# Last attention's bias stored once a query and added on GpSimd, and the last product split over two engines

## The chip, the cores and the metric

The kernel runs on one core of a Trainium2 chip, as one program in one launch. The metric is the device time of a whole execution, in microseconds (us), as the median of several executions. The engines are named as the profile names them: PE is the tensor engine (PEld its weight load), DVE the vector engine, ACT the scalar engine, POOL is GpSimd, and SP is the engine that issues the DMAs (SPq its queue).

## What is computed

Two blocks, one behind the other, in float32, for one sequence of 256 tokens of 1024 features. The first has two layers with grouped attention, neighbourhood attention and gates. The second has a feed-forward stage, a mixer, another feed-forward stage and an embedding step, and ends in an RMS norm. The change touches one part of the mixer, and the last norm. Cut to these:

```python
def dsa_attention(q, c_kv, q_idx, k_idx, w_idx, rel_bias):
    # per block of 128 queries
    score = jnp.einsum('bths,bth->bts', jax.nn.relu(dots), w)
    score = jnp.where(causal[None], score, -jnp.inf)
    _, sel = lax.top_k(score, top_k)                    # 64 keys of each query
    bias = rel_bias[t5_bucket(q_pos[None, :, None] - sel)]
    logits = einsum('bthc,btkc->bthk', qb, kv_sel) * (dc ** -0.5) + bias
    logits = jnp.where(valid, logits, -jnp.inf)
    probs = jax.nn.softmax(logits, axis=-1)
    return jnp.einsum('bthk,btkc->bthc', probs, kv_sel)

def rms_norm_2(x, g):
    return x * lax.rsqrt(jnp.mean(x * x, axis=-1, keepdims=True) + EPS) * g

def second_block(...):
    ...
    hn = rms_norm_2(h, ple_norm[i])
    h = h + jax.nn.sigmoid(hn @ ple_w_gate[i]) * (p[i] @ ple_w_proj[i])
    return rms_norm_2(h, final_norm)
```

The bias of a head depends only on the distance of query and key, and there are 8 heads (SH).

## The kernel before

**Weights.** All large weights come as one stream of units of 128x2048 numbers (`load_unit`, L691), which SP loads into a ring of three buffers `raw`. For each unit ACT makes `w_hi`, the rounded weights (`cut_to`, L831), and DVE or POOL makes `w_lo = raw - w_hi` in four pieces of 128x512 (DVE: `lo_to`, L1265; POOL: L814, for the units named in `POOLS`, among them "iq", "ms" and "yg"). PE multiplies three times for each block (hi x hi, hi x lo, lo x hi, L1988; for "gv" L2270) and so makes a "line", one tile of 128 features by 256 tokens. Most units hold two lines. A unit is loaded when `w_lo` of the unit three before it is done; its `w_hi` is made when PE is done with the lines of the unit three before it.

**Order.** Each engine has its own program, written out by hand, and runs it in order; the engines meet only at semaphores. In ACT's program, `cut_to(u)` stands at fixed places among other work and makes `w_hi` up to unit u.

**The bias row.** PE computes the bias by distance for 8 heads as one 8x512 tile, ACT copies it to `bias_row`, 8 partitions of `turned`. SP stores it to DRAM as `row_dram`, 8 rows of 2 KB (L750), behind the load of the unit of lines gv6 and gv7; the next load is that of unit iq0 (lines iq0 and iq1). In the stage of the levels that follows, PE makes the lines gv0 to gv7 and iq0 to iq3 two by two, with other products between them; ACT copies each gv line out of its bank (L1098), and PE's line gv(n+2) waits for the copy of gv(n).

**The choice.** `choose(t)` on DVE, for each of two query tiles t, keeps 64 keys of each query (MAX8 and MATCH_REPLACE8) and leaves `score[:, t]`, 0 for a chosen key and -1e30 for others.

**The last attention.** 16 jobs, (head, query tile), with 128 keys for tile 0 and 256 for tile 1. For job i:
- SP has loaded the bias of the head into one of two buffers `rbias` (`load_rbias`, L716). The source rows overlap: row p is `row_dram` shifted by p numbers, so the queries come in reversed order.
- PE: `dsa_scores(i)`, the score product (L2353), and onto it the product of the constant "flip" with `rbias` (L2355), which turns the order of the queries.
- DVE: `dsa_maxes(i)`, adds `score` (L1863), then the maximum, negated (L1864).
- ACT: `dsa_exps(i)`, the exponential with its sum (L1175).
- DVE: `dsa_shares(i)`, reciprocal (L1870) and normalisation (L1871).
- PE: `dsa_turn(i)`, transposes into the bank `turn` (L2364); ACT: `dsa_turned(i)` copies it out (L1183); PE: `dsa_values(i)` (L2373); ACT and DVE split the result of a head into hi and lo.

Between these run the lines of `DSA_FILLERS`: ms0 to ms7 in jobs 0 to 7, yg0 to yg7 in jobs 8 to 15. PE's order in step i is: score i, line i, turn i-1, values i-2. ACT's is: exponential i, then `cut_to` the unit two ahead of that of line i (so in even steps a `w_hi` of 1.9 us), for an "ms" line its tanh, then the copy of turn i-1. DVE's is: maximum i, shares i, the scaling or gating of line i (which frees its bank), and the lo part of a head.

**The end.** For each of 8 lines "pg", DVE scales the line, and one step later makes the new `h` (`embedded(m)`), ACT squares it, DVE adds the squares (`add_square`, L1304). PE sums over the partitions (`norm_sum`, L2016), ACT takes Ln and Exp, DVE makes three small steps (L1290, L1281, L1282) for the root's reciprocal and then eight products `wide = h * g * r` (L1951). SP stores them in four DMAs (L762).

```python
        def dsa_scores(i):
            ...
            pe.matmul(bank[:, 0:keys], dq[:, hd, t * P:(t + 1) * P], ckv[:, 0:keys], start=True, stop=False)
            pe.wait_ge(rbias_in[hd % 2], 16 * TILES * (hd // 2 + 1))
            pe.matmul(bank[:, 0:keys], const("flip"), rbias[:, hd % 2, t * P:t * P + keys], start=False,
                      stop=True).then_inc(score_done, 1)
```

Of the kernel before, what the change touches and what calls it, by code (L numbers as in the profile page):

```python
# [317 lines left out]
CONST, CONST_W = columns([("ident", P), ("flip", P), ("head_mean", P),  # L318
# [169 lines left out]
def hybrid_blocks_kernel(nc, weights, tokens, embeds, small_in, small2_in, rpb, consts_in, consts2_in, levels_in,  # L488
# [87 lines left out]
    rbias_in = [sem(f"rbias_in{i}") for i in range(2)]  # L576
# [8 lines left out]
    dq_ready, relued, scored = sem("dq_ready"), sem("relued"), sem("scored")  # L585
    od_hi_ready, od_ready = sem("od_hi_ready"), sem("od_ready")
# [4 lines left out]
    stored = sem("stored")  # L591

# [17 lines left out]
    row_dram = nc.dram_tensor("bias_by_distance", (SH, 2 * SEQ), F32).ap()  # L610
# [62 lines left out]
    rbias = a4.sb("rbias", [2, SEQ + P])  # L673
# [3 lines left out]
    bias_row = turned[0:SH].rearrange("p a b -> p (a b)")[:, SEQ:3 * SEQ]  # L677
    a3.close()
# [6 lines left out]
    def _(sp):  # L685
# [22 lines left out]
        def load_rbias(hd):  # L708

            if hd >= 2:  # L710

                sp.wait_ge(score_done, SCORE[("mixer", "dsa", hd - 2, TILES - 1)] + 1)
# [12 lines left out]
        for u in range(1, NU):  # L725
# [34 lines left out]
        for k in range(0, KT, 2):  # L760
            sp.wait_ge(out_ready, k + 2)
# [5 lines left out]
    def _(pool):  # L767
# [30 lines left out]

        means = False
# [16 lines left out]


    @block.scalar
    def _(act):
# [350 lines left out]
        def dsa_exps(i):  # L1170
# [5 lines left out]
                           accum_out=total[:, n % 2, 0:1]).then_inc(exped, 1)  # L1176
# [44 lines left out]

        def square_of_result(k):
# [3 lines left out]
        for m in range(KT):  # L1226
# [6 lines left out]
            if m:  # L1233
                square_of_result(m - 1)
        square_of_result(KT - 1)
        load_log_table(False)
# [4 lines left out]
    def _(dve):  # L1241
# [35 lines left out]
        def newton(r, v, mean, out_=None):  # L1277
# [4 lines left out]
            link(dve.scalar_tensor_tensor(r if out_ is None else out_, v, -3.0, r, ALU.add, ALU.mult))  # L1282

        def rstd_of(key, n, out_=None):
# [8 lines left out]
            newton(r, v, mean, out_)  # L1293
# [532 lines left out]
        def choose(t):  # L1826
# [13 lines left out]
            link(dve.tensor_tensor(own, own, const("later"), ALU.add))  # L1840
# [96 lines left out]
        for m in range(KT):  # L1937
# [612 lines left out]
```

## Time and profile before

| | |
|---|---|
| median of 3 executions | 1202.46 us (1201.43 to 1204.3) |
| profiled execution | 1199.7 us, its span 1197.9 us |
| mean granted clock of PE | 0.993 |
| PE busy in the span | 1149.3 us, 96% |
| DVE, ACT, POOL busy | 829.4, 602.7, 255.5 us |
| moved by DMA | 188.05 MB, 157 GB/s on average |

The profile is of one execution. Its span is the time between the first and the last instruction; the execution's own time is 1.8 us longer. A time such as "at 861.3" is counted from the span's start. In a row of the timeline the two first numbers are start and duration in us. Operations on one engine overlap a little: the next starts before the last one's end. A bracket at a row's end says how long the engine was idle before it and which operation ended that.

### The profile page before, as it was taken

To read this page: it belongs to the slowest core of one execution; us is meant where nothing else is said; L and a number is where in the kernel's file an instruction comes from. 1 tells how busy PE (TensorE), PEld (TensorE's weight loads), DVE (VectorE), ACT (ScalarE), POOL (GpSimd) and SP (SyncE) were. 2 spreads that over 40 slices of the span, in tenths; PEclk is the share of its full clock that TensorE was granted. 3 is DMA by queue.
4 is the path that set the end of the run, shared out by engine and by line. 5 is a ranking of instruction groups with operands and counts; after the bars stand their busy time and mean duration, and the time that the engine had idled before them with its cause. 6 is when DMAs were issued, how large, how long until landed. Compare 5 with 4: busy or idle time off the path is not lost.

```text
span 1197.9 us, 23145 instructions
## 1 busy us (share of the span) xinstructions
PE 1149.3 (96%) x9278; PEld 1121.2 (94%) x9278; DVE 829.4 (69%) x1801; ACT 602.7 (50%) x941; POOL 255.5 (21%) x213
## 2 busy tenths in 40 slices
PE   6999999999999998999999999999999999999996
PEld 6999999999999998999999899888899999999995
DVE  6954445879445477887766799577846877776667
ACT  6454545554555546454444553565454554444453
POOL 1065543200756514000000008300561000000000
PEclk9999999999999999999999999999999999999998
DMA  6743353356533633555455443224464555554551
GB/s 241 177 183 126 107 129 108 140 165 166 188 129 112 164 114 141 194 206 182 155 178 194 178 176 142 106 72 154 150 166 147 185 177 177 189 187 148 191 201 36
DMA packets 47978, 188.05 MB, mean 157 GB/s; under 512 B 20856, under 2 KB 24184, under 8 KB 29312
## 3 DMA queue, kind: packets, MB, share of 16 engines
q1 hardware_dynamic: 47872, 186.58, 46.7%
q8 instruction: 74, 1.21, 0.4%
q14 instruction: 32, 0.26, 0.1%
HBM read 185.50 MB, written 1.06 MB: 156 GB/s over the span
## 4 chain that ended last, share of the span: by engine, by line
PE 78%; DVE 14%; ACT 3%; issue 2%; DMA 1%; POOL 0%; SPq 0%; DVEq 0%; ACTq 0%
PE line L1988 48%; PE result L1988 17%; DVE w_lo L1265 4%; PE line L2270 1%; PE turn L2117 1%; PE result L2151 1%; ACT w_hi L831 1%; PE stat L2151 1%; PE score L2098 1%; PE score L2287 1%; PE score L2094 1%; DMA raw<-in_weights 1%; DMA rel<-in_rpb 1%; DVE wide L1547 1%; DVE prod L1544 1%
## 5 line engine op out<-in xcount | busy, mean ns | idle before, releaser
L831 ACT ACTIVATE w_hi<-raw 128x2048 fp32r<-128x2048 f32 (+2 forms) x178 | 321.9, 1810 | 112.6 <-PE line L1988 41.0
L814 POOL TENSOR_TENSOR w_lo<-raw,w_hi 128x512 fp32r<-128x512 f32 x168 | 227.5, 1386 | 572.5 <-ACT w_hi L831 572.5
L1265 DVE TENSOR_TENSOR w_lo<-raw,w_hi 128x512 fp32r<-128x512 f32 (+2 forms) x544 | 337.3, 665 | 4.8 <-ACT w_hi L864 2.6
L1988 PE MATMUL line<-x_hi,w_hi 128*128 128x256 f32 (+1 forms) x1080 | 320.0, 296 | 12.7 <-DVE x_lo L1311 8.5
L1988 PE MATMUL line<-x_hi,w_lo 128*128 128x256 f32 (+1 forms) x1080 | 308.3, 285 | 0.0
L1988 PE MATMUL line<-x_lo,w_hi 128*128 128x256 f32 (+1 forms) x1080 | 307.9, 285 | 0.0
L1988 PEld LDWEIGHTS line<-x_hi,w_hi 128*128 128x128 f32 x1080 | 205.7, 190 | 19.2 <-issue 13.0
L1988 PEld LDWEIGHTS line<-x_lo,w_hi 128*128 128x128 f32 x1080 | 205.2, 190 | 1.7
L1988 PEld LDWEIGHTS line<-x_hi,w_lo 128*128 128x128 f32 x1080 | 205.6, 190 | 0.0
L1988 PE MATMUL line<-y_hi,w_hi 128*128 128x256 f32 (+1 forms) x688 | 203.8, 296 | 1.8 <-DVE y_lo L1520 1.2
L1988 PE MATMUL line<-y_hi,w_lo 128*128 128x256 f32 (+1 forms) x688 | 194.7, 283 | 0.0
L1988 PE MATMUL line<-y_lo,w_hi 128*128 128x256 f32 (+1 forms) x688 | 194.4, 283 | 0.0
L1988 PEld LDWEIGHTS line<-y_hi,w_hi 128*128 128x128 f32 x688 | 129.8, 189 | 3.9 <-DVE y_lo L1520 1.4
L1988 PEld LDWEIGHTS line<-y_lo,w_hi 128*128 128x128 f32 x688 | 129.6, 188 | 1.5
L1988 PEld LDWEIGHTS line<-y_hi,w_lo 128*128 128x128 f32 x688 | 130.0, 189 | 0.0
L1988 PE MATMUL result<-x_hi,w_hi 128*128 128x256 f32 (+1 forms) x232 | 65.5, 282 | 0.0
L1988 PE MATMUL result<-x_lo,w_hi 128*128 128x256 f32 (+1 forms) x232 | 65.4, 282 | 0.0
L1988 PE MATMUL result<-x_hi,w_lo 128*128 128x256 f32 (+1 forms) x232 | 65.4, 282 | 0.0
L956 ACT ACTIVATE probs<-score,top 128x272 f32<-128x272 f32 (+1 forms) x66 | 32.2, 487 | 64.0 <-DVE top L1438 36.8
L1988 PE MATMUL result<-y_lo,w_hi 128*128 128x256 f32 x192 | 54.0, 281 | 0.0
L1988 PE MATMUL result<-y_hi,w_lo 128*128 128x256 f32 x192 | 54.0, 281 | 0.0
L1988 PE MATMUL result<-y_hi,w_hi 128*128 128x256 f32 x192 | 53.9, 281 | 0.0
(335 smaller groups left out, 2193.6 us busy)
## 6 DMA issues: line engine op xcount, KB each, us to landing
raw<-in_weights SPq DMA_DIRECT2D x145, 1024.0 KB, 4.8
raw<-in_weights SPq DMA_DIRECT2D x32, 704.0 KB, 4.1
rel<-in_rpb SPq DMA_DIRECT2D x64, 64.0 KB, 6.5
h<-in_tokens SPq DMA_DIRECT2D x2, 544.0 KB, 6.0
raw<-in_weights SPq DMA_DIRECT2D x2, 512.0 KB, 5.7
rbias<-bias_by_distance SPq DMA_DIRECT2D x8, 128.0 KB, 5.6
out<-wide SPq DMA_DIRECT2D x4, 256.0 KB, 2.2
consts<-in_consts SPq DMA_DIRECT2D x1, 832.0 KB, 6.7
```

The lines of the kernel that those rows point to most:

```text
L814: pool.tensor_tensor(w_lo[:, u % CUT, at], raw[:, u % RAW, at], w_hi[:, u % CUT, at].bitcast(F32), ALU.subtract).then_inc(lo_pool, 1)
L831: act.activation(w_hi[:, v % CUT, first:n], raw[:, v % RAW, first:n], ACT.Copy).then_inc(hi_cut, 1)
L956: act.activation(probs[0:m, place % 2, half * SECOND:half * SECOND + TOK], score_bank[s % 2][0:m, 0:TOK], ACT.Exp, bias=top[0:m, n % 2, 0: ...
L1265: dve.tensor_tensor(w_lo[:, u % CUT, at], raw[:, u % RAW, at], w_hi[:, u % CUT, at].bitcast(F32), ALU.subtract).then_inc(lo_cut, 1)
L1544: dve.scalar_tensor_tensor(prod[:, m % 2, 0:W], gate["b"][:, m, 0:W], 1.0, line_wait((name, "yb", m))[:, 0:W], ALU.add, ALU.mult).then_inc ...
L1547: dve.tensor_tensor(wide[:, m, 0:W], prod[:, m % 2, 0:W], gate["a"][:, m, 0:W], ALU.add).then_inc(full_ready, 1)
L1988: ins = pe.matmul(bank[:, 0:n], stay, move[:, first + k, 0:n], start=(k, m) == (0, 0), stop=(k, m) == (depth - 1, 2))
L2094: ins = pe.matmul(s[:, 0:TOK], qa[:, c, t * P:(t + 1) * P], ka_half[:, half * TOK:(half + 1) * TOK], start=True, stop=True)
L2098: ins = pe.matmul(s[:, 0:TOK], qb[:, c, t * P:(t + 1) * P], kb[:, c, half * TOK:(half + 1) * TOK], start=True, stop=True)
L2117: ins = pe.transpose(turn_bank[:, b * P:b * P + m], probs[0:m, place, first:first + P], ident[0:m, 0:m])
L2151: ins = pe.matmul(single_bank[pair % 2][:, cols], tn[:, b * P:(b + 1) * P], v[:, kt, cols], start=(half, kt) == (0, 0), stop=b == both)
L2270: ins = pe.matmul(bank, stay[:, k], move[:, k], start=(k, m) == (0, 0), stop=(k, m) == (KT - 1, 2))
```

## The change

- The store of the bias row now writes each head's row 128 times, once for each query of a tile: `row_dram` is 8 x 128 x 384 numbers. The source is `bias_row` broadcast over the middle dimension.
- `load_rbias` reads row p of a head's table at a shift of -p, with a pitch of 383 numbers, so the queries come in their own order. There are four buffers `rbias` instead of two (`RING` is 4), and the loads of four heads are issued ahead of unit mg2 instead of two. A later load waits for the maximum of the head four before it.
- "flip" is no more: neither the product in `dsa_scores` nor the constant.
- POOL adds `score`, the choice, to `rbias` (`bias_of`), in place. In POOL's program these additions stand behind the last piece of unit ms0 + n, for n = 1 to 7 (ms0 is the unit of lines ms0 and ms1): jobs 2n-2 and 2n-1 behind unit ms0 + n, and jobs 12 to 15 behind the last.
- DVE's `dsa_maxes` waits for that addition and for the score product, and makes sum and maximum in one operation; it leaves the sum negated, so ACT's exponential takes a scale of -1. The last operation of `choose` is signalled to POOL (`chosen`).
- At the end, `embedded(m)` comes in its own step, behind the addition of the square before it; ACT also makes `hg = h * g` (`gained`), and loads its table ahead of the last square; PE sums in two products, the last one straight from ACT's square; and the eight last products become four of 128x512, three on DVE and one (features 4 and 5) on POOL, which is stored last.

```diff
-            for t in range(TILES):
-                at = hd * 2 * SEQ + SEQ - (t + 1) * P
-                src = bass.AP(row_dram.tensor, at, [[1, P], [1, (t + 1) * P]])
-                sp.dma_start(rbias[:, hd % 2, t * P:t * P + (t + 1) * P], src).then_inc(rbias_in[hd % 2], 16)
+            for t in range(TILES):
+                at = hd * P * SPREAD + SEQ - t * P - 1
+                src = bass.AP(row_dram.tensor, at, [[SPREAD - 1, P], [1, (t + 1) * P]])
+                sp.dma_start(rbias[:, hd % RING, t * P:t * P + (t + 1) * P], src).then_inc(rbias_in[hd % RING], 16)
...
-                sp.dma_start(row_dram, bias_row).then_inc(row_stored, 16)
+                sp.dma_start(row_dram, bias_row[:, 0:SPREAD].unsqueeze(1).to_broadcast([SH, P, SPREAD])).then_inc(
+                    row_stored, 16)
...
-                load_rbias(0)
-                load_rbias(1)
-            if 2 <= u - UNIT[("mixer", "ms", 0)] - 1 < SH:
+                for hd in range(RING):
+                    load_rbias(hd)
+            if RING <= u - UNIT[("mixer", "ms", 0)] - 1 < SH:
...
+        def bias_of(i):
+            hd, t = DSA_JOBS[i]
+            at = rbias[:, hd % RING, t * P:t * P + (t + 1) * P]
+            pool.wait_ge(rbias_in[hd % RING], 16 * TILES * (hd // RING + 1))
+            pool.wait_ge(chosen, t + 1)
+            pool.tensor_tensor(at, at, score[:, t, 0:(t + 1) * P], ALU.add).then_inc(chosen_bias, 1)
...
                 pool.tensor_tensor(w_lo[:, u % CUT, at], raw[:, u % RAW, at], w_hi[:, u % CUT, at].bitcast(F32),
                                    ALU.subtract).then_inc(lo_pool, 1)
+                hd = u - UNIT[("mixer", "ms", 0)]
+                if 1 <= hd < SH and end == BLOCKS[u]:
+                    for i in range(TILES * (hd - 1), TILES * (hd + (hd == SH - 1))):
+                        bias_of(i)
...
+        pool.wait_ge(hg_ready, KT)
+        pool.wait_ge(last_root, 1)
+        by = rstd[:, STAT[("final1", "norm")] % 2, 0:SEQ].unsqueeze(1).to_broadcast([P, 2, SEQ])
+        pool.tensor_tensor(wide[:, 4:6, 0:SEQ], hg[:, 4:6], by, ALU.mult).then_inc(out_pool, 1)
...
             bank = score_bank[s % 2][:, 0:keys]
+            dve.wait_ge(chosen_bias, i + 1)
             dve.wait_ge(score_done, s + 1)
-            link(dve.tensor_tensor(bank, bank, score[:, t, 0:keys], ALU.add))
-            dve.tensor_reduce(top[:, n % 2, 0:1], bank, AX.X, ALU.max, negate=True).then_inc(maxed, 1)
+            dve.tensor_tensor_reduce(bank, bank, rbias[:, hd % RING, t * P:t * P + keys], scale=-1.0, scalar=3.0e38,
+                                     op0=ALU.add, op1=ALU.min, accum_out=top[:, n % 2, 0:1]).then_inc(maxed, 1)
...
             if m:
-                embedded(m - 1)
-            if m >= 2:
-                add_square("final1", m - 2, m - 2, SEQ)
-        embedded(KT - 1)
-        add_square("final1", KT - 2, KT - 2, SEQ)
-        add_square("final1", KT - 1, KT - 1, SEQ)
-        dve.wait_ge(h_ready, H_BATCH["embed"] + KT)
-        r = rstd_of(("final1", "norm"), SEQ)
-        for k in range(KT):
-            dve.scalar_tensor_tensor(wide[:, k, 0:SEQ], h[:, k, 0:SEQ], operand("g_final1")[:, k:k + 1], r, ALU.mult,
-                                     ALU.mult).then_inc(out_ready, 1)
+                add_square("final1", m - 1, m - 1, SEQ)
+            embedded(m)
+        dve.wait_ge(hg_ready, KT)
+        r = rstd_of(("final1", "norm"), SEQ, last=True)
+        by = r.unsqueeze(1).to_broadcast([P, 2, SEQ])
+        for k in (0, 2, 6):
+            dve.tensor_tensor(wide[:, k:k + 2, 0:SEQ], hg[:, k:k + 2], by, ALU.mult).then_inc(out_ready, 1)
...
-            pe.matmul(bank[:, 0:keys], dq[:, hd, t * P:(t + 1) * P], ckv[:, 0:keys], start=True, stop=False)
-            pe.wait_ge(rbias_in[hd % 2], 16 * TILES * (hd // 2 + 1))
-            pe.matmul(bank[:, 0:keys], const("flip"), rbias[:, hd % 2, t * P:t * P + keys], start=False,
+            pe.matmul(bank[:, 0:keys], dq[:, hd, t * P:(t + 1) * P], ckv[:, 0:keys], start=True,
                       stop=True).then_inc(score_done, 1)
...
-        norm_sum("final1", SEQ)
+        pe.wait_ge(summed, SUMMED["final1"] + KT - 1)
+        pe.matmul(stat_bank[:, 0:SEQ], mean_dm[:, :], sum_of["final1"][0][:, 0:SEQ], start=True, stop=False)
+        pe.wait_ge(squares_ready, SQUARES[("final1", "norm")] + KT)
+        pe.matmul(stat_bank[:, 0:SEQ], mean_dm[:, :], square_of["final1"][:, (KT - 1) % 2, 0:SEQ], start=False,
+                  stop=True).then_inc(stat_done, 1)
```

## Rows read from the trace of the kernel before

**Rows 1.** The page: the span, and part 1, busy time of each engine.
```profile
span 1197.9 us, 23145 instructions
PE 1149.3 (96%) x9278; PEld 1121.2 (94%) x9278; DVE 829.4 (69%) x1801; ACT 602.7 (50%) x941; POOL 255.5 (21%) x213
```
**Rows 2.** Timeline, last attention: start us, us, engine, line, operation, out<-in, count.
```profile
861.10 0.40 PE L2353 MATMUL score<-ckv,wide 128*128 128x128 f32 x2
861.33 0.39 PE L2355 MATMUL score<-rbias,consts 128*128 128x128 f32 x2
...
865.24 0.60 PE L2353 MATMUL score<-ckv,wide 128*128 128x256 f32 x2
865.67 0.59 PE L2355 MATMUL score<-rbias,consts 128*128 128x256 f32 x2
```
**Rows 3.** Timeline of ACT and POOL, last attention's first jobs.
```profile
859.91 0.37 ACT L1175 ACTIVATE probs<-score,top 128x128 f32<-128x128 f32 x1 [4.71 <-DVE top L1864]
860.26 1.90 ACT L831 ACTIVATE w_hi<-raw 128x2048 fp32r<-128x2048 f32 x1
862.24 10.11 POOL L814 TENSOR_TENSOR w_lo<-raw,w_hi 128x512 fp32r<-128x512 f32 x8 [6.23 <-ACT w_hi L831]
```
**Rows 4.** One line of the kernel (L796): POOL's 128x256 additions, durations in ns.
```profile
L796 POOL TENSOR_TENSOR prod<-prod,th x14: 728/742/1257, 455.1 to 477.6; 128x256 f32<-128x256 f32 x14
```
**Rows 5.** Timeline of DVE, the first maximum.
```profile
859.25 0.30 DVE L1863 TENSOR_TENSOR score<-score,root 128x128 f32<-128x128 f32 x1
859.58 0.29 DVE L1864 TENSOR_REDUCE top<-score 128x1 f32<-128x128 f32 x1
```
**Rows 6.** Timeline of PE and ACT: ACT's copy before turn 12, turns 12 and 14.
```profile
905.22 0.37 ACT L1183 ACTIVATE turned<-turn 128x256 f32<-128x256 f32 x1
908.89 0.27 PE L2364 MATMUL turn<-consts,probs 128*128 128x128 f32 x1
916.89 0.27 PE L2364 MATMUL turn<-consts,probs 128*128 128x128 f32 x1
```
**Rows 7.** Timeline of the DMA queue: the bias row's store and the next load.
```profile
702.38 0.38 SPq L750 DMA_DIRECT2D bias_by_distance<-turned  x1
707.51 0.36 SPq L691 DMA_DIRECT2D raw<-in_weights  x1
```
**Rows 8.** Stretches: start:end, us, busy of each engine (instructions), PEclk, DMA share, GB/s.
```profile
706.50:709.20 2.70, 2.70 (x26) 2.70 (x25) 2.48 (x5) 2.17 (x4) 0.00 (x0) 1.00 0.20 36
709.20:712.00 2.80, 2.80 (x27) 2.80 (x26) 2.61 (x5) 1.09 (x1) 0.00 (x0) 1.00 0.83 339
817.00:819.00 2.00, 2.00 (x18) 1.75 (x17) 1.22 (x3) 0.81 (x3) 0.00 (x0) 1.00 1.02 61
1194.00:1197.00 3.00, 0.00 (x0) 0.00 (x0) 1.35 (x4) 0.00 (x0) 0.00 (x0) 0.50 1.01 341
```
**Rows 9.** Timeline of ACT and PE behind the load of 707.51.
```profile
715.84 1.90 ACT L831 ACTIVATE w_hi<-raw 128x2048 fp32r<-128x2048 f32 x1
720.07 0.47 ACT L1098 ACTIVATE gv<-line,scale_t 128x256 f32<-128x256 f32 x1 [2.33 <-PE line L2270]
725.99 0.39 PE L2270 MATMUL line<-w_hi,x_hi 128*128 128x256 f32 x1 [1.34 <-DVE w_lo L1265]
```
**Rows 10.** Stretch in which PE starts again after idling (columns as in rows 8).
```profile
477.90:481.40 3.50, 2.92 (x10) 2.58 (x11) 0.81 (x2) 1.43 (x1) 0.72 (x3) 0.51 0.00 0
```
**Rows 11.** Timeline of DVE: a 128x512 product alone and beside POOL.
```profile
710.44 0.68 DVE L1741 TENSOR_TENSOR gate_q<-wide,fall 128x512 f32<-128x512 f32 x1
717.89 1.77 DVE L1741 TENSOR_TENSOR gate_q<-wide,fall 128x512 f32<-128x512 f32 x1
```
**Rows 12.** Timeline, the end of the kernel: ACT, DVE and the DMA queue.
```profile
1187.88 1.28 ACT L844 ACT_TABLE_LOAD   x1
1192.10 3.25 DVE L1951 SCALAR_TENSOR_TENSOR wide<-h,small,rstd 128x256 f32<-128x256 f32 x8
1193.00 2.75 SPq L762 DMA_DIRECT2D out<-wide  x4
```

More of the change, by code:

```diff
@@ L317 @@
 SMALL2, SMALL2_W = columns([("gla_gain", KT), ("ckv_gain", 1), ("alpha_b", GH), ("alpha_w", GH * GDK), ("rel", SH)])
-CONST, CONST_W = columns([("ident", P), ("flip", P), ("head_mean", P),
+CONST, CONST_W = columns([("ident", P), ("head_mean", P),
                           ("rot", P), ("cos", TOK), ("sin", TOK), ("window", GRID_W)])
@@ L575, in hybrid_blocks_kernel @@
     row_ready, row_stored = sem("row_ready"), sem("row_stored")
-    rbias_in = [sem(f"rbias_in{i}") for i in range(2)]
+    rbias_in = [sem(f"rbias_in{i}") for i in range(RING)]
     ckv_raw, ckv_ready = sem("ckv_raw"), sem("ckv_ready")
@@ L608, in hybrid_blocks_kernel @@
                    od_ready=od_ready, pp_ready=pp_ready, pg_raw=pg_raw)
-    row_dram = nc.dram_tensor("bias_by_distance", (SH, 2 * SEQ), F32).ap()
+    SPREAD = 3 * P
+    row_dram = nc.dram_tensor("bias_by_distance", (SH, P, SPREAD), F32).ap()
     a1 = Alloc(nc)
@@ L672, in hybrid_blocks_kernel @@
     od_lo = a4.sb("od_lo", [SH, SEQ], F32R)
[L673 removed]
+    rbias = a4.sb("rbias", [RING, SEQ + P])
     score = root[:, :, 0:SEQ]
@@ L677, in hybrid_blocks_kernel @@
     bias_row = turned[0:SH].rearrange("p a b -> p (a b)")[:, SEQ:3 * SEQ]
+    a3.close()
+    a3 = Alloc(nc)
+    hg = a3.sb("hg", [KT, SEQ])
     a3.close()
@@ L754, in _ @@
                 sp.wait_ge(gg_ready, KT)
-                load_rbias(0)
-                load_rbias(1)
-            if 2 <= u - UNIT[("mixer", "ms", 0)] - 1 < SH:
+                for hd in range(RING):
+                    load_rbias(hd)
+            if RING <= u - UNIT[("mixer", "ms", 0)] - 1 < SH:
                 load_rbias(u - UNIT[("mixer", "ms", 0)] - 1)
-        for k in range(0, KT, 2):
-            sp.wait_ge(out_ready, k + 2)
+        for n, k in enumerate((0, 2, 6, 4)):
+            if k == 4:
+                sp.wait_ge(out_pool, 1)
+            else:
+                sp.wait_ge(out_ready, n + 1)
             sp.dma_start(out[:, k:k + 2], wide[:, k:k + 2, 0:SEQ]).then_inc(stored, 16)
@@ L1220, in _, with gained @@
         root_of(("embed", "norm"), SEQ)
+        def gained(k):
+            act.activation(hg[:, k], h[:, k, 0:SEQ], ACT.Copy,
+                           scale=operand("g_final1")[:, k:k + 1]).then_inc(hg_ready, 1)
         def square_of_result(k):
@@ L1234, in _ @@
                 square_of_result(m - 1)
+            if m >= 2:
+                gained(m - 2)
+        load_log_table(False)
         square_of_result(KT - 1)
-        load_log_table(False)
+        gained(KT - 2)
+        gained(KT - 1)
         root_of(("final1", "norm"), SEQ)
@@ L1275, in lo_after, with newton, rstd_of @@
             lo_to(end + (LO_END[min(u + 2, NU - 1)] - end) * at // lines)
-        def newton(r, v, mean, out_=None):
+        def newton(r, v, mean, out_=None, last=False):
             mean(r)
             link(dve.tensor_tensor(v, v, r, ALU.mult))
-            link(dve.scalar_tensor_tensor(r if out_ is None else out_, v, -3.0, r, ALU.add, ALU.mult))
-        def rstd_of(key, n, out_=None):
+            ins = dve.scalar_tensor_tensor(r if out_ is None else out_, v, -3.0, r, ALU.add, ALU.mult)
+            if last:
+                ins.then_inc(last_root, 1)
+                dve.wait_ge(last_root, 1)
+            else:
+                link(ins)
+        def rstd_of(key, n, out_=None, last=False):
             s = STAT[key] % 2
@@ L1291, in mean @@
                 dve.wait_ge(stat_read, STAT[key] + 1)
-            newton(r, v, mean, out_)
+            newton(r, v, mean, out_, last)
             return r if out_ is None else out_
@@ L1838, in choose @@
             link(dve.tensor_scalar(score[:, t, 0:keys], work[:, t, 0:keys], TAKEN / 2, NEG, ALU.is_gt, ALU.mult))
-            link(dve.tensor_tensor(own, own, const("later"), ALU.add))
+            dve.tensor_tensor(own, own, const("later"), ALU.add).then_inc(chosen, 1)
         for n, (t, hd) in enumerate((t, hd) for t in range(TILES) for hd in range(SH)):
@@ L2485, in constants @@
     put("ident", np.eye(P))
-    put("flip", np.eye(P)[::-1])
     put("head_mean", (p[:, None] // HD == p[None] // HD) / HD)
```

9 lines of the change are left out of this document (6 added, 3 removed).

## The prediction, made blind

> **What bounds the kernel now.** I read the page first: the tensor engine is busy 96% of the span, the vector engine 69%, GpSimd 21% [rows 1]. So time leaves only where TensorE does less while nothing else becomes last, and time arrives wherever an edit makes TensorE wait. Then I went to the three places that the diff touches: the store of the bias row (at 702 us of the span), the last attention (850 to 920 us) and the end (from 1187 us). In the waits of the last attention TensorE loses only 1.6 us, once, at the turn of job 0; otherwise it streams, two jobs in 8.00 us (turns 12 and 14, [rows 6]). At the end TensorE is done and a chain ACT, DVE, DMA queue is left [rows 12].
>
> **The "flip" product removed (L2355).** Each of 16 jobs loses one product of the same shape as the score product before it, and that one holds TensorE 0.23 us for 128 keys and 0.43 us for 256 (start to start, [rows 2]). Eight of each: 5.3 us, or 0.66 us per two jobs, so TensorE alone would need 8.00 - 0.66 = 7.34 us per two jobs. The flips of jobs 0 and 1 lie ahead of the turn where TensorE already waits for the choice, so they give nothing; there one DVE operation less helps by 0.33 us (L1863 start to L1864 start, [rows 5]). If nothing else moved, the stage would gain 7 x 0.66 + 0.33 = 4.9 us.
>
> **The bias added by GpSimd.** POOL makes w_lo of the unit weights here, and the new additions for jobs 2k and 2k+1 are queued behind the four pieces of unit ms0+k+1 (ms0 being the first "ms" unit). Those pieces need w_hi of that unit, which ACT, in order, makes only behind the exponential of job 2k-2. And the exponential of job 2k now needs POOL's addition. That closes a ring that did not exist before: exponential of an even job, w_hi, four pieces, addition, maximum, exponential of the next even job. One round: exponential to w_hi 0.35, w_hi 1.90, handover 0.08, four pieces 10.11 / 2 = 5.06 (all [rows 3]), the 128x128 addition, a handover of 0.04 (my estimate, half of the one above), maximum to exponential 859.91 - 859.58 = 0.33 [rows 3, 5]. The addition isn't in the trace. A 128x256 one takes 0.74 us [rows 4], and a 128x512 piece 1.26 (10.11 / 8, [rows 3]); a line through these gives 0.48 for 128. Its bounds are half of 0.74 and 0.74 itself. The round is 8.24 us, against 7.34 us for TensorE: the ring is slower and sets the pace.
> It runs six times (jobs 0 to 12; units up to the last "yg"). Exponential 0 starts at 859.91 - 0.33 = 859.58 [rows 3, 5], exponential 12 at 859.58 + 6 x 8.24 = 909.0. Turn 12 then also needs the turn bank, freed by ACT's copy of turn 11, which is queued behind exponential 12 and its w_hi: 0.35 + 1.90 + 0.37 = 2.6 us (the copy: [rows 6]), so turn 12 starts at 911.6 instead of 908.89, and with 7.34 us to turn 14 the stage ends at 918.9 instead of 916.89 [rows 6]: +2.0 us, where 4.9 us seemed to be saved. With the addition at 0.37 it is +1.4, at 0.74 +3.6. Waiting behind POOL's additions are only its own next pieces, whose w_hi comes later anyway; waiting behind DVE's new wait are the normalisation and the line's scaling, which is what TensorE's turns see.
> The wait for the bias itself costs nothing: four heads are loaded some 40 us ahead, and the loads of later heads wait for maxima long past.
>
> **The stored table.** The store grows from 16 KB to 8 x 128 x 384 x 4 = 1.57 MB, and every one of its 1024 rows of 1536 bytes is read from one of only eight SBUF partitions. It is queued on SP at 702.38, behind a weight load, and the next weight load (unit iq0) follows at 707.51 [rows 7] on the same DMA queue. The DMA engines are nearly idle from 706.5 to 709.2 (36 GB/s), and the load then moves in 2.8 us [rows 8]. How long does the store take? The trace has no store of this kind. From below: the final result is written in packets of the same order at 341 GB/s [rows 8]: 4.6 us. From above: the loads of the bias read 128 overlapping rows out of one 2 KB row, so many requests go to the same few bytes, and there all the DMA engines are busy (share 1.02) at 61 GB/s [rows 8]: 25.8 us. The new store also asks 128 times for the same bytes, so I take the latter; on one queue the weight load waits for it.
> Who waits for that load: w_hi of iq0 stands in ACT's order at 715.84, in front of the copy of gv4 (720.07), which frees the bank for TensorE's line gv6, which started at 725.99 [rows 9]. New: store from 706.5 to 732.3, load 2.8, w_hi 1.9, copy 0.47, three handovers 0.3: gv6 at 737.8, which is 11.8 us late. The point from which it costs anything is a store of 706.5 + d + 5.5 = 726.0, d = 14.0 us; a store of 4.6 us costs 0. After such an idle time the clock comes back slowly: behind a shorter idle time TensorE ran at 0.51 of full speed, the 1.2 GHz level, from its restart at 478.5 to 481.4 [rows 10]; 2.9 us at half speed lose 1.4 us. Sum: +13.2 us, between 0 and, at 50 GB/s, 19.
> A page makes the long store likelier. "SBUF — State Buffer", section "Door 1: The DMA port swizzle", of the Trainium skill says that DMA reaches SBUF through 16 ports of about 27 GB/s each, and that four neighbouring partitions share one, with 27.6 GB/s measured on partitions 0 to 3. Eight partitions would be two ports, 54 GB/s and 28.9 us, and the sum of this part 16.3 instead of 13.2. No row here has a DMA on so few partitions.
>
> **The end.** The last eight products take 3.25 us [rows 12]. New: three 128x512 products on DVE and one on POOL. DVE's takes 0.68 us alone and 1.77 beside a POOL operation on SBUF [rows 11]. POOL's takes about 1.3 (as a piece), so one DVE product is the slow one: 1.77 + 2 x 0.65 = 3.0 us, and then two DMA issues of 0.4 in place of one, since the pair of POOL is issued last: +0.1. If they don't collide: 3 x 0.65 + 0.4 = 2.35, -0.9. The log table is loaded ahead of the last square instead of behind it (1.28 us from 1187.88, [rows 12]); ACT is free about 1.3 us earlier, so the square ends about 0.4 us later, and DVE's last addition of 0.4 falls away: 0. I take 0 for the end, -0.9 to +0.3.
>
> **At no cost.** "flip" out of the constants: 64 KB less in a load that nobody waits for. Eight issues instead of four ahead of unit mg2: 1.6 us of the SP queue, hidden by weight loads that are made two units ahead.
>
> **Sum.** +13.2 + 2.0 + 0 = +15.2 us. The profiled execution took 1199.7 us (span 1197.9 and 1.8 around it); it becomes 1214.9. The median of the runs, 1202.46, lies 2.8 higher and becomes 1217.7.
>
> **Rivals.**
> (a) The port rule holds as the page has it. Its mechanism here is the same queue, with a store of 28.9 us: the gap grows by 3.1 us, 1220.8. For it: only eight partitions; against: no row. 0.26.
> (b) The store is hidden: it runs near the 341 GB/s of the result, any length under 14 us. Only the ring and the end remain, 1202.46 + 2.0 = 1204.5. For it: all 16 engines and the idle time at 706.5; against: the 61 GB/s stretch. 0.16.
> (c) Faster: POOL's additions come in time and TensorE keeps the pace. It takes a round below 7.34 us, and the store under 14 us; then the last attention gives 4.9 us, 1197.6, and up to 0.9 more at the end. Against it: w_hi and the pieces alone take 6.96 us, by [rows 3], so it would need another order than the one written. 0.12.
> (d) A long store, but no ring: 13.2 - 4.9 = +8.3, 1210.8. 0.05.
>
> **How the numbers follow.** The forecast has 0.36, the others as above, and 0.05 are left for what I don't see. The measurement can tell about 0.2% (2.4 us) from no change. Slower by more: 0.36 + 0.26 + 0.05, most of the rest and the upper edge of (b), 0.74; within: the body of (b), 0.13; faster: (c) and a little, 0.13. The range takes in (b), (d), the forecast and (a) with a store near 32 us: 1203 to 1224, 0.83 of the chance.
>
> **What would show it.** The store: DMA engines busy at 50 to 64 GB/s from 706 to past 730, ACT's w_hi of iq0 waiting for the DMA of raw, one TensorE gap of 11 to 16 us ahead of gv6 and PEclk at 0.5 behind it. The ring: ACT's even exponentials 8.1 to 8.4 us apart, DVE's maxima waiting for POOL, TensorE's turns of even jobs each some 0.9 us late. The end: one DVE product near 1.7 us, the rest near 0.7. The prediction is wrong in the large if the DMA rate in that stretch is above 110 GB/s, and wrong in the small if the rounds are near 7.4 us.

## The result, and the profile after

The changed kernel takes 1224.05 us (median, 1222.4 to 1225.4), the kernel before 1201.95 beside it: ratio 1.0184, 95% interval 1.0162 to 1.0206, so 22.1 us slower. The forecast was 1217.7. The direction, the two mechanisms and their places were right. The store was priced too cheap, and the time lies just above the upper end of the range (1224).

The profile's page of the changed kernel: the span, the busy times, and TensorE's granted clock in 40 slices.

```profile
span 1222.3 us, 23135 instructions
PE 1151.3 (94%) x9248; PEld 1122.2 (92%) x9248; DVE 821.4 (67%) x1795; ACT 604.5 (49%) x949; POOL 265.6 (22%) x230
...
PEclk9999999999999998999999897999999999999998
```

Against [rows 1]: 30 products fewer, yet TensorE is busy 2.0 us more, because it ran more of its work at the slow clock. The busy time of no engine explains the 24.4 us by which the span grew, so most of them are in waits. The list of waits between 700 and 760 us has them (who waits, for whom, us in total, times, longest):

```profile
ACT w_hi L860 <- DMA raw<-in_weights: 24.1, 1, 24.1
PE line L2312 <- ACT gv L1127: 17.8, 1, 17.8
```

The same two in the timeline (start, us, engine, line, operation; in brackets the idle time before it), with the DMA queue's own rows:

```profile
706.13 0.83 SPq L758 DMA_DIRECT2D bias_by_distance<-turned  x1
711.45 7.11 SPq L699 DMA_DIRECT2D raw<-in_weights  x1
...
743.81 1.91 ACT L860 ACTIVATE w_hi<-raw 128x2048 fp32r<-128x2048 f32 x1 [24.12 <-DMA raw<-in_weights]
745.63 0.46 ACT L1127 ACTIVATE gv<-line,scale_t 128x256 f32<-128x256 f32 x1
...
746.23 0.55 PE L2312 MATMUL line<-w_hi,x_hi 128*128 128x256 f32 x1 [17.82 <-ACT gv L1127]
```

And in stretches of 4 us (busy time of each engine with its instructions, PEclk, DMA share, GB/s):

```profile
712.00:716.00 4.00, 4.00 (x37) 4.00 (x36) 3.78 (x7) 2.05 (x2) 0.00 (x0) 1.00 0.46 50
724.00:728.00 4.00, 4.00 (x37) 4.00 (x36) 2.01 (x4) 0.00 (x0) 0.00 (x0) 1.00 0.76 170
736.00:740.00 4.00, 0.00 (x0) 0.00 (x0) 0.00 (x0) 0.00 (x0) 0.00 (x0) 0.50 0.44 49
740.00:744.00 4.00, 0.00 (x0) 0.00 (x0) 0.00 (x0) 0.19 (x1) 0.00 (x0) 0.50 0.51 204
748.00:752.00 4.00, 4.00 (x30) 4.00 (x29) 3.97 (x3) 1.67 (x2) 4.00 (x4) 0.81 0.00 2
```

This is the chain of the prediction, link for link: the store, then the weight load behind it, w_hi of iq0, the copy of gv4, line gv6 (compare [rows 7 to 9]). Where only the store runs, DMA moves 49 to 50 GB/s with a share of 0.45: a bit under half of the engines busy. By its own packets (the trace's only ones of 1536 bytes between 700 and 760 us) the store runs from 710.1 to 741.0: 30.9 us, 51 GB/s. Its issue was at 706.13, and 3.8 us of that start are older than the store (below). From 719 to 732 us weight loads move beside it (177, 170 and 180 GB/s in stretches of 4 us from 720 on), and still the one that w_hi needs is complete only when the store is gone: the rate is 204 from 740 on. Gv6 starts at 746.23 instead of 725.99, and TensorE runs slowly until about 749.5.

The last attention, ACT's exponentials of four even jobs (6, 8, 10 and 12), and one round of GpSimd and the vector engine:

```profile
905.85 0.37 ACT L1204 ACTIVATE probs<-score,top 128x128 f32<-128x128 f32 x1 [3.14 <-DVE top L1907]
914.09 0.37 ACT L1204 ACTIVATE probs<-score,top 128x128 f32<-128x128 f32 x1 [2.00 <-DVE top L1907]
922.32 0.37 ACT L1204 ACTIVATE probs<-score,top 128x128 f32<-128x128 f32 x1 [4.39 <-DVE top L1907]
930.56 0.37 ACT L1204 ACTIVATE probs<-score,top 128x128 f32<-128x128 f32 x1 [4.39 <-DVE top L1907]
...
914.45 1.91 ACT L860 ACTIVATE w_hi<-raw 128x2048 fp32r<-128x2048 f32 x1
916.43 5.05 POOL L834 TENSOR_TENSOR w_lo<-raw,w_hi 128x512 fp32r<-128x512 f32 x4 [2.07 <-ACT w_hi L860]
921.44 1.15 POOL L817 TENSOR_TENSOR rbias<-rbias,root 128x128 f32<-128x128 f32 x2
921.93 0.30 DVE L1907 CUSTOM_DVE_ANT_0 score<-score,rbias 128x128 f32<-128x128 f32 x1 [3.42 <-POOL rbias L817]
```

The rounds shown are 8.24, 8.23 and 8.24 us (all six, from 881.08 to 930.56, are 8.25 on average), and each link can be read off: exponential 914.09, w_hi 914.45, pieces 916.43, additions 921.44, maximum 921.93, next exponential 922.32.

The end: products of the vector engine and of GpSimd, and the issues of the four stores.

```profile
1215.32 2.96 DVE L1993 TENSOR_TENSOR wide<-hg,rstd 128x512 f32<-128x512 f32 x3
1215.43 1.70 POOL L845 TENSOR_TENSOR wide<-hg,rstd 128x512 f32<-128x512 f32 x1 [283.47 <-DVE rstd L1319]
1216.04 3.19 SPq L774 DMA_DIRECT2D out<-wide  x4
```

Where the 24.4 us of span went, by how late the same instructions are against the kernel before: 3.8 us by 690 us, ahead of every changed part (0.85 of it by 670 us, the rest below); 20.2 at gv6; 21.7 at 760 us, behind the gap; 21.2 at exponential 0 (881.08 against 859.91); 23.75 at the last line's scaling (1208.82 against 1185.07); 24.4 at the end. So 17.4 us arise between 690 us and the last attention, 2.6 from there to the last line, 0.65 in the end.

One row was a surprise, the stretch from 682 to 688 us of the changed kernel:

```profile
682.00:688.00 6.00, 6.00 (x26) 5.62 (x26) 1.78 (x6) 2.39 (x2) 0.00 (x0) 0.50 0.44 164
```

and of the kernel before:

```profile
682.00:688.00 6.00, 6.00 (x51) 5.95 (x50) 4.63 (x10) 4.89 (x5) 0.00 (x0) 1.00 0.35 145
```

TensorE is busy throughout and yet at half clock: 25 products fewer in 6 us, 2.9 us lost, before the store is even issued.

### The profile page after: what moved, and what is told of

Same layout as the page of the kernel before. It is cut to its first block, busy times and chain, and to the rows that moved or that the text cites. A ratio compares the mean times of both kernels' runs of the same rounds, so it can differ in the third digit from the quotient of the medians.

```text
span 1222.3 us, 23135 instructions
## 1 busy us (share of the span) xinstructions
PE 1151.3 (94%) x9248; PEld 1122.2 (92%) x9248; DVE 821.4 (67%) x1795; ACT 604.5 (49%) x949; POOL 265.6 (22%) x230
## 4 chain that ended last, share of the span: by engine, by line
PE 72%; DVE 12%; ACT 4%; DMA 4%; issue 4%; POOL 3%; SPq 0%; DVEq 0%; ACTq 0%; POOLq 0%
PE line L2030 44%; PE result L2030 17%; DVE w_lo L1302 4%; DMA raw<-in_weights 3%; POOL w_lo L834 2%; ACT w_hi L860 1%; PE turn L2159 1%; PE result L2193 1%; PE stat L2193 1%; PE line L2312 1%; PE score L2140 1%; PE score L2136 1%; DMA rel<-in_rpb 1%; DVE wide L1589 1%; PE score L2329 1%
```

## The experiments

Three questions: is it the store, and what makes it slow; is it the ring; is any of it the end or chance. All times are medians, ratios are against the kernel before on the same chip.

**The store alone.**

```diff
                 sp.dma_start(row_dram, bias_row).then_inc(row_stored, 16)
+                sp.dma_start(table_dram, bias_row[:, 0:SPREAD].unsqueeze(1).to_broadcast([SH, P, SPREAD])).then_inc(
+                    row_stored, 16)
```

> The kernel before, with one thing added: behind the 16 KB store of the bias row (702 us) it also stores the table of the changed kernel, 8 x 128 x 384 floats out of the same eight partitions, into memory that nothing reads; the bias is read as before and the flip product stays. My theory is that this store alone makes most of the loss: in the changed kernel it held SP's queue from about 706 to 741 us, 14 us of that hidden, so I expect +17 to +18.5 us over the kernel before, ratio 1.014 to 1.0155, DMA engines at about 50 GB/s for some 31 us, and one gap of TensorE of about 17 us ahead of line gv6. Rival: the loss came from the store together with the changed rest (the GpSimd additions, the end, the fall of the clock at 681 us); then this kernel loses clearly less, +5 to +13 us. The clock of TensorE fell to 0.5 at 682 to 688 us in the changed kernel, ahead of the store, and cost 2.9 us; nothing that this kernel adds lies ahead of that, so if the fall is the change's own it is not here (clock 1.0 in that stretch), and if it is chance it may be in any kernel.

Measured: 1220.19 against 1201.17 us, ratio 1.0167 (1.0140 to 1.0194). TensorE's one gap, in this kernel:

```profile
745.92 0.55 PE L2274 MATMUL line<-w_hi,x_hi 128*128 128x256 f32 x1 [17.95 <-ACT gv L1102]
```

The store alone carries 19 of the 22 us. That is a little over the 17 to 18.5 expected. Its profile says the same: the instructions are 3.3 us late at 700 us and 22.5 at 760. The fall of the clock at 682 us is here too, so it isn't the change's.

**Half of it.** The same kernel, with `P // 2` for `P` in the table and in the repeat.

> The kernel before with half of the added store: each of the eight rows 64 times instead of 128, so 0.79 MB out of the same eight partitions. At the 50 GB/s of the whole one it takes 15.5 us. The prediction said that the weight load behind it has 14.0 us of room. Theory: only what lies above that costs, 1.5 us, with little or no fall of the clock behind it, so +1 to +3 us (ratio 1.001 to 1.0025) where the whole store cost 19. Rival: the cost goes with the bytes (they take DMA time and SBUF ways from everything): half of 19, +9 us, ratio 1.008.

Measured: 1203.48 against 1200.90, ratio 1.0033 (1.0016 to 1.0049); by the medians 2.6 us, by the ratio 4.0 (1.9 to 5.9). A cost by bytes, half of 19, is outside. In its profile the store's packets run 14.9 us, from 709.4 to 724.2. TensorE starts gv6 at 729.46, 3.5 us later than in the kernel before; 3.25 of that stood already at 685 us (w_hi at 688.64 against 685.39, after the fall of the clock), and by 760 us it is 4.8. So in that execution the half store cost 1.6 us, where 1.5 was expected. At 810 us the difference is 3.2 again, but that is the other kernel's doing: in the profile of the kernel before, TensorE's clock fell to half at 795 us and cost 1.6 us, and here it did not. The kernel before, and this one:

```profile
796.00:800.00 4.00, 4.00 (x24) 4.00 (x24) 2.81 (x7) 2.24 (x7) 0.00 (x0) 0.65 0.01 2
...
800.00:804.00 4.00, 4.00 (x37) 4.00 (x36) 3.64 (x10) 1.43 (x5) 0.00 (x0) 1.00 0.00 0
```

There is a point from which a store decides, and it is near the 14 us read out of [rows 7 to 9]. What makes the rest of the 2.6 us isn't settled; the kernel before varies by more from run to run (1197.6 to 1204.8).

**128 source partitions.** The bias product takes each head's column 16 times.

```diff
-    bias_row = turned[0:SH].rearrange("p a b -> p (a b)")[:, SEQ:3 * SEQ]
+    bias_row = turned.rearrange("p a b -> p (a b)")[:, SEQ:3 * SEQ]
...
-                sp.dma_start(row_dram, bias_row[:, 0:SPREAD].unsqueeze(1).to_broadcast([SH, P, SPREAD])).then_inc(
-                    row_stored, 16)
+                sp.dma_start(row_dram.rearrange("h (s r) x -> (h s) r x", s=P // SH),
+                             bias_row[:, 0:SPREAD].unsqueeze(1).to_broadcast([P, SH, SPREAD])).then_inc(row_stored, 16)
...
-    put("rel", a["rel_bias_2"])
+    put("rel", np.repeat(a["rel_bias_2"], P // SH, 1))
```

> The changed kernel with the same table stored out of 128 partitions instead of eight: the bias product takes each head's column 16 times, so that its result has 16 equal rows a head, ACT copies all 128 partitions, and each partition is stored eight times. Same 1.57 MB, same 1024 rows of 1536 bytes, outermost dimension 128 instead of 8. Three accounts of the slow store: (ports) eight neighbouring partitions are the limit: the store now runs at 200 to 340 GB/s, 5 to 8 us, below the 14 us that are hidden, and the kernel gains 17 to 18.5 us over the changed one, about 1206 us. (engines) the transfer was cut over eight of the DMA engines: now 16, 100 GB/s, 15 to 16 us, gain 16 to 17 us, about 1207.5 us, and the plateau near 100 GB/s. (rows) 1024 rows of 1536 bytes or the writes cost it: still 50 GB/s, and the time stays at 1224 us.

Measured: 1204.68, ratio 1.0036 (1.0019 to 1.0053). The list of DMA issues (KB each, us from issue to landing):

```profile
bias_by_distance<-turned SPq DMA_DIRECT2D x1, 1536.0 KB, 9.8
```

Same bytes, same 1024 rows, 9.8 us with a weight load ahead of it on the same engines (its own packets take 5.0 us, 712.2 to 717.1): the rows and their size are not the limit. The "engines" account as it was written falls too, since it wanted 100 GB/s and 15 to 16 us for the store. The gain of 19.4 us (1224.05 less 1204.68, not of one chip session) is over both accounts' figures and doesn't tell them apart. The cleaner test is to change only where the rows lie, in the next three.

**Sixteen neighbouring partitions**, two equal rows a head, outermost dimension 16.

> The changed kernel, its store reading 16 neighbouring partitions (two equal rows a head, each stored 64 times), outermost dimension 16. Four groups of four neighbours instead of two: about 100 GB/s, 15 to 16 us for the store, near the 14 us of room, so 1205 to 1210 us. If what limited the changed kernel was instead only the number of DMA engines, it would be at 100 GB/s too; if it was the number of rows and their size, 50 GB/s and 1223 us. What it tells beside the run with eight rows apart is whether the rate goes with the groups of four (twice the changed kernel's 49 GB/s) and whether 16 engines slowed by full ways hold the weight loads up more than eight do.

Measured: 1208.74, ratio 1.0070 (1.0054 to 1.0085). While only the store runs:

```profile
712.00:714.00 2.00, 2.00 (x19) 2.00 (x19) 1.94 (x4) 0.52 (x1) 0.00 (x0) 1.00 0.90 98
716.00:718.00 2.00, 2.00 (x19) 2.00 (x19) 1.80 (x3) 0.80 (x2) 0.00 (x0) 1.00 0.91 98
```

98 GB/s from four groups of four neighbours, 49 from two. The share is 0.90 instead of 0.45: all 16 engines occupied, and each as slow as before.

**Eight partitions, four apart** (0, 4, ..., 28), outermost dimension 8. This differs from the changed kernel's store in nothing but the place of the rows.

```diff
-                sp.dma_start(row_dram, bias_row[:, 0:SPREAD].unsqueeze(1).to_broadcast([SH, P, SPREAD])).then_inc(
+                sp.dma_start(row_dram, bias_row[0:4 * SH:4, 0:SPREAD].unsqueeze(1).to_broadcast([SH, P, SPREAD])).then_inc(
```

> The changed kernel, its store reading eight partitions four apart (0, 4, ..., 28) with the bias product's result repeated four times; outermost dimension 8. The run with partitions 16 apart lost 6.9 us to the kernel before, the one with 128 partitions 3.5 us, the changed one with eight neighbours 22. (neighbours share) only groups of four neighbouring partitions share a way, so four apart is as good as 16 apart or better: 1204 to 1208.5 us. (distance) rows must lie far apart, in different quarters of the memory: four apart is worse than 16 apart, 1209 us or more. By the table in the Trainium skill, SBUF - State Buffer, section Door 1: The DMA port swizzle, partitions 0, 4, ..., 28 lie on eight ports and 0, 16, ..., 112 on four, which would make this run the faster of the two, near the 1204.7 us of the 128 partitions.

Measured: 1202.72, ratio 1.0013 (0.9999 to 1.0027), and, while only the store runs:

```profile
708.00:710.00 2.00, 2.00 (x20) 2.00 (x20) 1.66 (x4) 1.85 (x2) 0.00 (x0) 1.00 0.50 186
```

Eight engines again (share 0.50), but 186 GB/s instead of 49. So the limit of the changed kernel's store is in the source: each group of four neighbouring partitions gives about 24.5 GB/s (49 / 2, 98 / 4), and eight groups, four apart, give nearly eight times that (186). The time is a little better than the 1204 to 1208.5 us expected. The number of engines is set apart from it, by the outermost dimension. The Trainium skill has both: "SBUF — State Buffer", section "Door 1: The DMA port swizzle", lets four neighbours share a port (27.6 GB/s measured there on partitions 0 to 3, a tenth less, 24.5, here), and "DMA: Bandwidth & Descriptors", section "Why a DMA increments its semaphore by 16 and not by 1", takes the number of engines from the slowest dimension. The shares 0.45, 0.50 and 0.90 agree.

**Eight partitions, 16 apart** (0, 16, ..., 112).

> As the run with 128 source partitions, but the store reads eight of them, 16 apart (0, 16, 32, ...), and its outermost dimension is 8, as in the changed kernel. It differs from the changed kernel's store in nothing but where the eight rows lie. (ports) eight partitions 16 apart no longer share a way into SBUF: the store is two times faster or more, 100 GB/s and over, 8 to 15.5 us, time 1206 to 1208 us. (engines) still eight DMA engines, with their busy share at half: 47 to 51 GB/s, 30 to 31 us, time 1223 to 1225 us. (rows) the same 1223 to 1225 us; the run with 128 partitions tells it from engines.

Measured: 1208.05, ratio 1.0058 (1.0040 to 1.0077); gv6 waits 1.92 us and a bit more is lost behind it. Much better than neighbours, as the "ports" account wants, but worse than four apart. The Trainium skill's table ("SBUF — State Buffer", section "Door 1: The DMA port swizzle") would put these rows on four ports, as many as the run with 16 neighbours has. The times of the two agree (1208.05 and 1208.74), and so do the lengths: the store's own packets run 14.2 us here and 14.3 there. Its rate starts higher, 184 to 192 GB/s from 712.5 to 715 us and 115 at 716 to 717. From then on it is that of four ports: between 718 and 724 us, beside weight loads,

```profile
DMA packets 492, 1.54 MB, mean 257 GB/s; under 512 B 8, under 2 KB 372, under 8 KB 372
```

364 of these packets have the store's 1536 bytes, 93 GB/s; four times 24.5 is 98. Why the first 3 us are faster stays open.

**Another queue.** The changed kernel's own store, taken out of SP's program and issued by ACT right behind its copy of the row.

```diff
+        act.wait_ge(row_ready, 1)
+        act.dma_start(row_dram, bias_row[:, 0:SPREAD].unsqueeze(1).to_broadcast([SH, P, SPREAD])).then_inc(
+            row_stored, 16)
```

> The changed kernel, its store out of eight neighbouring partitions unchanged, but issued by ACT right behind its copy of the bias row (about 690 us) and so on ACT's DMA queue instead of SP's. Two accounts of why the weight load waited for the store. (queue order) transfers of one queue are worked off in order: on another queue the loads pass the store, and the kernel loses nothing by it: 1203 to 1207 us, as the run with 128 partitions. (shared engines) the eight DMA engines that carry the store are held by it whatever the queue, and each weight load needs all 16: the load of a unit still takes up to 30 us; since the store starts some 15 us earlier, the loss falls from 19 to somewhere between 5 and 19 us, 1210 to 1224 us, with the load of a unit at 10 us or more in that stretch instead of 5.

Measured: 1214.72, ratio 1.0114 (1.0089 to 1.0139). What each queue moved (packets, MB, share of 16 engines), between 700 and 704 us:

```profile
DMA packets 192, 0.69 MB, mean 173 GB/s; under 512 B 8, under 2 KB 132, under 8 KB 132
q10 hardware_dynamic: 124, 0.19, 43.7%
q1 hardware_dynamic: 66, 0.48, 29.8%
```

The store (q10) keeps its eight engines at 0.19 MB in 4 us, 48 GB/s; the loads (q1) pass on the others, but each load also has a part on the eight, and w_hi waits 19.0 us for one. It costs 10 us more than with 128 partitions (1214.72 against 1204.68), though it is issued 23 us earlier. That is what the expectation's "shared engines" gives (1210 to 1224), not "queue order" (1203 to 1207). So it isn't the queue that blocks, it is the engines. In the prediction's picture ("on one queue the weight load waits for it") that link was too narrow.

**The additions one unit earlier**, with 128 source partitions.

```diff
-                    for i in range(TILES * (hd - 1), TILES * (hd + (hd == SH - 1))):
+                    for i in range(TILES * (hd - (hd == 1)), TILES * (hd + 1)):
```

> The changed kernel with the store out of 128 partitions and, in GpSimd's order, the bias additions one unit earlier: behind the pieces of unit ms0+k stand those of jobs 2k and 2k+1 (in the changed kernel they stand behind the pieces of ms0+k+1); only the first two jobs keep their place. My theory of the last attention is the ring exponential, w_hi, four pieces, addition, maximum: with the additions a round earlier the ring is open, even exponentials come 7.3 to 7.5 us apart instead of 8.2, and the stage takes 4.5 to 7 us less than in the run with 128 partitions alone: about 1199 to 1202 us if that one has 1206. Rival: GpSimd isn't what sets the pace, the round is ACT's and the vector engine's own work (exponentials, copies, w_hi, line scaling); then the rounds stay at 8.0 us or more and the time is within 1 us of the run with 128 partitions alone.

Measured: 1198.11, ratio 0.9973 (0.9959 to 0.9986); 6.6 us less than with 128 partitions alone. Its even exponentials:

```profile
876.05 0.37 ACT L1204 ACTIVATE probs<-score,top 128x128 f32<-128x128 f32 x1 [0.76 <-DVE top L1907]
883.36 0.37 ACT L1204 ACTIVATE probs<-score,top 128x128 f32<-128x128 f32 x1 [0.76 <-DVE top L1907]
890.71 0.37 ACT L1204 ACTIVATE probs<-score,top 128x128 f32<-128x128 f32 x1 [0.76 <-DVE top L1907]
```

Rounds of 7.31 and 7.35 us, where the prediction had 7.34 for TensorE alone; TensorE's turns of jobs 2 to 14 are 7.31 to 7.35 us apart, all six times. From exponential 0 to the last copy of the stage it is 53.8 us (865.15 to 918.98) instead of 60.6 (864.70 to 925.29). The ring was real, and the order of two items in GpSimd's program made it.

**The same again**, beside the two with other ends.

> The same kernel as the earlier run with 128 partitions and early additions, beside the two with other ends: it should again be 2 to 4 us faster than the kernel before (0.9973 then). The other part of the question is TensorE's clock. It fell to half in stretches that differ from execution to execution (at 682 us in four of the profiles so far, not in two); if these falls are chance they are elsewhere again in this second profile of the same kernel.

Measured: 1198.04, ratio 0.9967 (0.9954 to 0.9979). The gain stands. And the clock, 682 to 688 us, in the first profile of this kernel:

```profile
682.00:688.00 6.00, 6.00 (x42) 5.06 (x41) 4.50 (x13) 3.15 (x4) 0.00 (x0) 1.00 0.50 175
```

and in the second:

```profile
682.00:688.00 6.00, 6.00 (x25) 4.70 (x24) 3.30 (x10) 2.40 (x2) 0.00 (x0) 0.60 0.46 175
```

Over all 14 profiles of this study the clock fell in that stretch in nine and not in five, with no relation to the edit. It is chance, since the same kernel has it in one execution and not in the other, and the 2.9 us of it in the 24.4 between the two spans are no part of the change. The difference of the medians, 22.1, is 2.3 smaller than 24.4.

**The new end alone**, on the kernel before.

> The kernel before with only the new end: gain taken into hg by ACT, log table loaded ahead of the last square, the last square summed by TensorE, three paired products on the vector engine and one on GpSimd. In the changed kernel the stretch from the last line scaling to the end of the span is 13.5 us where it was 12.8 before. Theory 1 (the prediction's step, between -0.9 and +0.3, now moved up by what the profile after shows): +0.3 to +0.8 us, so the ratio is 1.000 to 1.001 and can't be told from none. Theory 2 (the end is a clear part of the loss, or of the 3.5 us that the run with 128 partitions still lost): +1.5 us or more, ratio above 1.001.

Measured: 1203.10 against 1202.49, ratio 1.0001 (0.9989 to 1.0013). Nothing that can be told. From the scaling of the last line to the vector engine's first use of the sum it is 5.64 us (1187.89 to 1193.53), and in the kernel before 5.64 too (1185.07 to 1190.71): the new order brings nothing there. (In the changed kernel it is 5.12 us, because its last sum still ran at full clock: 0.70 us against 1.22 here.) From the first product to the end of the span it is 6.4 us instead of 5.8.

**The old end** under the wide, early kernel.

> The kernel with the table stored out of 128 partitions and the additions a unit earlier, with the end of the kernel before put back (eight products on the vector engine, four stores in order). By theory 1 it is 0.3 to 0.8 us faster than with the new end, some 0.04%, not to be told in the times but seen in the profile: last line scaling to end of span 12.8 us instead of 13.5. By theory 2 it is 1.5 us or more faster.

Measured: 1196.69, ratio 0.9954 (0.9938 to 0.9970), the fastest kernel of the study by its median; its interval overlaps that of the one with the new end. In the profile the end takes 13.0 us from the last scaling, against 13.9 (second profile of the other). By the medians the old end is 1.35 us faster, between the two theories (0.8 and 1.5).

**All four pairs on the vector engine.**

> The same kernel with the new end, but GpSimd's pair given to the vector engine: four paired products of 128x512, stores in order. The prediction said that the vector engine's product takes 1.77 us beside a GpSimd operation and about 0.65 alone, so 3.0 us for its three (2.96 measured) becomes 4 x 0.65 = 2.6 us and every product is near 0.65. If the shared port costs what I think, the end is 0.4 us shorter than with GpSimd; if the three products are slow for another reason (each near 0.99 us), four of them take 3.9 us and the end is 0.5 to 0.9 us longer.

Measured: 1198.55, ratio 0.9961 (0.9947 to 0.9975), and

```profile
1190.78 2.50 DVE L1986 TENSOR_TENSOR wide<-hg,rstd 128x512 f32<-128x512 f32 x4
```

Four products in 2.50 us without GpSimd, three in 2.96 beside it: GpSimd's help is worth less than it costs. The end is 13.1 us in this profile instead of 13.9, but in the times the two can't be told apart (1198.55 and 1198.04). A part of the tail that no product shortens is the way out of the last 1 MB, by estimate 3.1 us: the rate is 341 GB/s in the kernel before [rows 8], and in the run with the new end alone

```profile
1198.50:1200.50 2.00, 0.00 (x0) 0.00 (x0) 0.00 (x0) 0.00 (x0) 0.00 (x0) 0.50 1.01 343
```

## Why the prediction was right or wrong

- **Chain of the store: right.** The place, the order store, load, w_hi, copy, gv6, and that there is one gap were as forecast; its length, 17.8 us, is over the 11 to 16 that were said. The load behind the store took 2.8 us, as forecast (741.0 to w_hi at 743.8). The 14 us of room held for half a store: 14.9 us long, it cost 1.6 us in the profile and 2.6 by the medians, where a cost by bytes would be 9.5.
- **Rate of the store: the step that failed, a term of the sum that was sized too small.** I had two rows to go by, 341 and 61 GB/s, and took 61 because the bias loads also ask many times for the same bytes. That likeness was the wrong one: rows repeated as often from eight groups of four partitions run at 186. The length was 25.8 us in the sum and 30.9 in the trace (710.1 to 741.0; the start is the forecast 706.5 and the 3.8 us of lateness from before). The term was +13.2, and the store alone measured 19.0 (ratio interval: 17 to 23); so of the 6.4 us between forecast and result, 5.8 are this term. The prediction had it as its bound: "at 50 GB/s, 19".
- **Rival (a)** was the true cause: few partitions share a way. Its 1220.8 was 3.2 us short: 2.0 of that is the rate (30.9 us instead of 28.9), the rest lies in the other terms and in the scatter of the medians. I gave it 0.26 and my own analogy 0.36. A stated mechanism about just this shape should have weighed more than the nearest row by look.
- **"On one queue": too narrow.** On another queue, and issued 23 us earlier, the same store still cost some 10 us.
- **Flip product, 0.66 us per two jobs: right.** With the ring open the rounds are 7.31 to 7.35 us (7.34).
- **Ring: right.** 8.24 us forecast, 8.25 measured on average; GpSimd's addition for 128 keys 0.49 (forecast 0.48). From exponential 0 to turn 14 it is 59.5 us (881.08 to 940.62), forecast 59.3, and 57.0 in the kernel before. So behind exponential 0 the stage grew by 2.6 us, where the forecast was 2.3 (and 2.0 with an exponential 0 that comes 0.33 earlier). Opened, the ring gives back 6.6 us (2.0 + 4.9 forecast).
- **Rival (c)** asked for "another order than the one written". That order exists, and with the store out of 128 partitions it gives 1198.1 (forecast 1197.6).
- **End: near nothing, as said, but on small grounds.** Three products 2.96 us (3.0), GpSimd's 1.70 (1.3 assumed). I put the end at 0, -0.9 to +0.3; it is +0.6 in the profiles, over the upper bound, and in the times it can't be told from none (interval -0.11% to +0.13%). What I left out is that the way out of 1 MB takes about 3.1 us (an estimate: 1.05 MB at 341 GB/s) of the tail whoever makes the products; that this is why they gained nothing is argued, not shown.
- **Slow clock behind the gap, 1.4 us: right** (half speed from 746.2 to about 749.5, 1.6 us).

By terms in medians: store 19.0, ring and the rest 3.5 (the run with 128 partitions, which still has both), sum 22.5 for the 22.1 measured. The run with rows four apart has ring and end too and costs only 1.7, so this second term is known no better than 1.7 to 3.5 (forecast 2.0).

## What to carry to other kernels

Before a small tile is stored many times, ask from how many groups of four partitions it is read and what its outermost dimension is. The groups must also be the right ones: eight groups four partitions apart ran at 186 GB/s, eight that are 16 apart took as long as four neighbouring groups. A product that repeats its stationary columns spreads the rows at no cost that shows, and took away the 19 us of loss. A slow transfer blocks every transfer that shares its engines, whatever the queue, so price it as a wait of the next weight load and look for the room in front of that. When a helper engine takes over a step in a loop, write down the ring that it closes and see whether the item can stand one round earlier: here one line of order was worth 6.6 us, twice the 3.1 us that the change gains once both faults are mended.

## What the runs showed of the hardware

- A store of 1.57 MB out of SBUF in rows of 1536 bytes moved 49 GB/s from 8 neighbouring partitions, 98 from 16, and 186 from eight that are four apart. From eight that are 16 apart it took 14.2 us, as from 16 neighbours (14.3).
- The DMA engines that carry a slow store count as busy (share 0.45 and 0.90), and a weight load with a part on them is complete only when that part has landed, on the store's queue (w_hi waits 24.1 us) and on another (19.0 us).
- TensorE's clock fell to half while it was 100% busy, at the end of a stretch of products with few rows (16 x 256 and 32 x 512, from 679 us), in nine of 14 profiled executions; in the other five it stayed at full behind the same products. In the changed kernel's it cost 2.9 us.
- One 128x512 product of the vector engine takes about 0.62 us alone (2.50 / 4); three take 2.96 us while GpSimd works on SBUF for 1.70 of them.
